# A three-block transformer kernel: the decay matmul's operands padded to 128 rows, and turned 32x32 blocks carried across quadrants by DMA instead of ScalarE

## The reference

```python
def swiglu(h, w_gate, w_up, w_down):
    return (jax.nn.silu(h @ w_gate) * (h @ w_up)) @ w_down
...
        dmat = b[..., :, None] - b[..., None, :] + lii[..., None, :]   # mLSTM, per head
        m_t = jnp.maximum(inter, jnp.max(dmat, axis=-1))
        w_intra = jnp.exp(dmat - m_t[..., None])
        s = jnp.einsum('bhtd,bhsd->bhts', qi, ki) * w_intra
...
    y = jax.nn.sigmoid(o.astype(F32)) * ht * jax.nn.silu(z.astype(F32))
    return y.astype(h.dtype) @ w_out
```

## Time and profile before

| | |
|---|---|
| median of 3 runs (lowest, highest) | 2404.92 us (2404.87, 2405.07) |
| profiled execution, its own time | 2404.78 us |
| its span | 2403.0 us |
| busy: PE, PEld, DVE, ACT, POOL | 99%, 81%, 73%, 55%, 2% |
| granted clock of TensorE | 0.999 of full speed |
| DMA | 578 MB, mean 241 GB/s; 71.5% of the 16 engines on SP's queue |

### The profile page before, as it was taken

How to read it: one execution, slowest core, us unless ns; L and a number is a source line. 1 busy time by engine, 2 the same in 40 slices (tenths; PEclk the granted TensorE clock), 3 DMA queues, 4 the chain that set the end, 5 groups by cost and what they waited for, 6 DMA issues and landing times.

```text
span 2403.0 us, 30577 instructions
## 1 busy us (share of the span) xinstructions
PE 2384.5 (99%) x11017; PEld 1944.2 (81%) x11017; DVE 1747.5 (73%) x2438; ACT 1312.8 (55%) x1913; POOL 44.3 (2%) x67
## 2 busy tenths in 40 slices
PE   9999999999999999999999999999999999999998
PEld 7777888888888888778888888888888778888887
DVE  8885778677787776668778677677776676666665
ACT  6665465545563555545545544555455576655553
POOL 1100000000000000000000000000000000000000
PEclk9999999999999999999999999999999999999999
DMA  8445888788889896567777787777777557776654
GB/s 298 146 132 172 269 294 308 256 305 301 286 313 311 286 316 229 163 222 242 240 238 232 244 273 241 239 239 236 243 245 239 155 186 264 251 240 215 227 194 136
DMA packets 161830, 578.14 MB, mean 241 GB/s; under 512 B 18288, under 2 KB 20592, under 8 KB 161680
## 3 DMA queue, kind: packets, MB, share of 16 engines
q1 hardware_dynamic: 160432, 572.64, 71.5%
q0 software_dynamic: 1104, 3.28, 0.5%
q10 hardware_dynamic: 144, 0.26, 0.0%
HBM read 574.01 MB, written 2.10 MB: 240 GB/s over the span
## 4 chain that ended last, share of the span: by engine, by line
PE 94%; DVE 2%; ACT 2%; issue 1%; DMA 1%; POOL 0%; SPq 0%; DVEq 0%; ACTq 0%
PE PS L1173 30%; PE PS L1175 30%; PE PS L1174 30%; DVE WL L2219 1%; ACT WH L1570 1%; PE PS L916 1%; DMA X<-in_x 0%; PE PS L811 0%; PE PS L884 0%; DVE X L2186 0%; PE PS L1006 0%; PE PS L1074 0%; PE PS L1026 0%; PE PS L1027 0%; PE PS L1023 0%
## 5 line engine op out<-in xcount | busy, mean ns | idle before, releaser
L2219 DVE TENSOR_TENSOR WL<-W,WH 128x1024 fp32r<-128x1024 f32 x814 | 988.9, 1222 | 506.4 <-ACT WH L1570 500.1
L1570 ACT ACTIVATE WH<-W 128x1024 fp32r<-128x1024 f32 x814 | 854.9, 1058 | 720.4 <-PE PS L1175 682.5
L1173 PE MATMUL PS<-WH,XTH 128*128 128x512 f32 x2144 | 853.5, 398 | 3.2 <-DVE XTL L1725 1.2
L1175 PE MATMUL PS<-WH,XTL 128*128 128x512 f32 x2144 | 835.7, 390 | 0.0
L1174 PE MATMUL PS<-WL,XTH 128*128 128x512 f32 x2144 | 835.2, 390 | 0.0
L1173 PEld LDWEIGHTS PS<-WH,XTH 128*128 128x128 f32 x2144 | 402.8, 188 | 93.8 <-issue 10.4
L1175 PEld LDWEIGHTS PS<-WH,XTL 128*128 128x128 f32 x2144 | 402.4, 188 | 85.4
L1174 PEld LDWEIGHTS PS<-WL,XTH 128*128 128x128 f32 x2144 | 402.9, 188 | 83.7 <-issue 3.8
L1173 PE MATMUL PS<-WH,YTH 128*128 128x512 f32 x1120 | 440.2, 393 | 3.5 <-DVE WL L2219 2.4
L1175 PE MATMUL PS<-WH,YTL 128*128 128x512 f32 x1120 | 436.1, 389 | 0.0
L1174 PE MATMUL PS<-WL,YTH 128*128 128x512 f32 x1120 | 436.0, 389 | 0.0
(11 more groups left out here) (287 smaller groups left out, 1182.2 us busy)
## 6 DMA issues: line engine op xcount, KB each, us to landing
W<-in_vec SPq DMA_DIRECT2D x192, 512.0 KB, 4.4
W<-in_avoz SPq DMA_DIRECT2D x192, 512.0 KB, 4.5
W<-in_wg SPq DMA_DIRECT2D x88, 512.0 KB, 5.1
W<-in_wu SPq DMA_DIRECT2D x88, 512.0 KB, 4.8
W<-in_wd SPq DMA_DIRECT2D x88, 512.0 KB, 4.9
W<-in_gate SPq DMA_DIRECT2D x64, 512.0 KB, 4.4
W<-in_aqk SPq DMA_DIRECT2D x64, 512.0 KB, 4.4
W<-in_aout SPq DMA_DIRECT2D x64, 512.0 KB, 4.4
```

The source lines that it names most:

```text
L1173: e.matmul(p, x, WH[:, g % NH, j], start=first, stop=False)
L1175: i = e.matmul(p, y, WH[:, g % NH, j], start=False, stop=last)
L1570: e.activation(WH[:, n % NH], W[:, i % NW], ACT.Copy).then_inc(s_hi, 1)
L2219: e.tensor_tensor(l, src, h.bitcast(F32), ALU.subtract).then_inc(s_lo, 1)
```

## The change

- `M2` and `nsel` have 128 rows instead of 64 (the added rows are zero), and the decay matmul uses them all. DVE instead of ACT writes the high part of M2, straight after the scan that makes MM; the decay matmul of head 0 stands three ticks earlier.
- `TQ` and `MT` get the layouts [p, b, j, t, r] and [p, a, j, t, r]: what goes from quadrant a to b is one run of 1 KB in each partition. The transposes write TQ with strides; the pair copies and low halves read MT and write YTH and YTL with strides (runs of 32 elements). With a scale, the low halves are 8 instructions of 128 elements a partition for 4 of 256.
- The 16 ACT copies of each of the 23 chunks are gone. SP issues 16 transfers, `carry`, each from 32 partitions of TQ to 32 partitions of MT, 1 KB a partition. They come in two parts of 8. `carry_points` places part 0 ahead of stream tile low+7 and part 1 ahead of low+8, where low is the last tile that DVE has lowered when it issues the second transpose. So the wait of part 0 on s_tq stands between two weight issues.
- ACT waits on s_mt >= 256 per chunk before the pair copies: 7 ticks behind the second transpose's tick for ffn (26th tick) and mix, 9 and more for keys, where one copy of 128x1024 then fills KT. DVE's low halves come a tick behind the pairs. DVE waits on s_mt before it writes TQ again; tasks that reuse MID or G1 wait on s_tq instead of s_mt.

```diff
+    for what, *a in score(plan):
+        if what in ("slot", "lower", "fold"):
+            low = max([low] + list(plan.lower[a[0]]))
+        elif what == "start" and a[0] in TURNED:
+            due.append(tick + TURNED[a[0]])
+        elif what == "tick":
+            tick += 1
+            while tick in due:
+                due.remove(tick)
+                number += 1
+                for part in range(2):
+                    points.setdefault(low + NW + 1 + part, []).append((number, part))
...
-        M2 = sb("M2", [64, 384], F32R)
-        nsel = sb("nsel", [64, 8], F32R)
-        MT = sb("MT", [128, 4, 256])
-        TQ = sb("TQ", [128, 2, 512])
+        M2 = sb("M2", [128, 384], F32R)
+        nsel = sb("nsel", [128, 8], F32R)
+        MT = sb("MT", [128, 4, 4, 2, 32])
+        TQ = sb("TQ", [128, 4, 4, 2, 32])
...
-                yield from ticks(0 if h else 3)
                 w.wait_ge(s_mm, 2)
                 w.wait_ge(s_nsel, 4)
-                e.matmul(b[:, 0:384], nsel[:, h:h + 1].to_broadcast([64, 128]), M2[:], start=True, stop=False)
+                e.matmul(b[:, 0:384], nsel[:, h:h + 1].to_broadcast([128, 128]), M2[:], start=True, stop=False)
...
-                yield from ticks(6 if h else 3)
+                yield from ticks(6)
...
             def pairs_T(number, k0, scale):
 
-                w.wait_ge(s_mt, number)
+                w.wait_ge(s_mt, 256 * number)
...
-                yield from ticks(19)
-                yield from quadrants(TQ_FFN + f + 1, MT, 4 if f == 10 else 2, s_mt)
+                yield from ticks(25)
                 w.wait_ge(s_unit, free)
-                yield from pairs_T(MT_FFN + f + 1, 4 * slot, None)
+                yield from pairs_T(TQ_FFN + f + 1, 4 * slot, None)
...
-                yield from blocks_T(MID)
-                yield from ticks(5 if f == 10 else 9)
+                yield from blocks_T(TQ_FFN + f + 1, MID)
+                yield from ticks(7)
                 yield from pair_lows(4 * slot, None)
...
-                yield from ticks(3)
                 w.wait_ge(s_gate, 8)
+                w.wait_ge(s_nsel, 4)
+                e.tensor_copy(M2[0:8, 0:256], MM)
+                e.tensor_copy(M2[0:8, 256:384], MM[:, 128:256]).then_inc(s_mm, 1)
                 w.wait_ge(s_mm, 1)
...
+            def carry(number, part):
+
+                w.wait_ge(s_tq, number)
+                if number > TQ_KEYS + 1:
+                    w.wait_ge(s_kq, number - TQ_KEYS - 1)
+                for a in (2 * part, 2 * part + 1):
+                    for b in range(4):
+                        e.dma_start(MT[32 * b:32 * b + 32, a].rearrange("p j t r -> p (j t r)"),
+                                    TQ[32 * a:32 * a + 32, b].rearrange("p j t r -> p (j t r)")).then_inc(s_mt, 16)
+
             for i, (kind, what, src) in enumerate(stream):
+                for number, part in points.get(i, ()):
+                    carry(number, part)
```

More of the change, by code:

```diff
@@ L487, in score, with carry_points @@
     yield from outproj("Y", fours(YT_BAND), 8, "bout", split=last_rows)
+def carry_points(plan):
+    points, due = {}, []
+    tick = low = number = 0
+    for what, *a in score(plan):
[10 more added lines that the diff above has]
+                    points.setdefault(low + NW + 1 + part, []).append((number, part))
+    return points
 def attention_steps(qready, at, turned):
@@ L1408, in gates @@
                 e.activation(gt, gt2, ACT.Ln, bias=onesf[:, 0:1]).then_inc(s_gact, 1)
[L1409 to L1414, removed]
+                yield from ticks(9)
                 w.wait_ge(s_gate, 9)
@@ L1451, in mix @@
                 if h:
-                    w.wait_ge(s_mt, MT_MIX + h)
+                    w.wait_ge(s_tq, TQ_MIX + h)
                 for t in range(2):
@@ L1458, in mix @@
                 e.activation(SG[:, 512:1024], Gb[ends[3][0]][1][:, :], ACT.Sigmoid).then_inc(s_mixa, 1)
-                yield from ticks(5)
-                yield from quadrants(TQ_MIX + h + 1, MT, 2, s_mt)
+                yield from ticks(10)
                 base = CGH + 4 * h - 4 * (h % 4)
                 w.wait_ge(s_unit, free)
-                yield from pairs_T(MT_MIX + h + 1, 4 * (h % 4), lambda kt: cols[:, base + kt:base + kt + 1])
+                yield from pairs_T(TQ_MIX + h + 1, 4 * (h % 4), lambda kt: cols[:, base + kt:base + kt + 1])
             def qc(n, par, g):
@@ L1475, in keys @@
                 qc(j, par, g)
-                yield from ticks(3 if j else 16)
+                yield from ticks(11 if j else 24)
                 w.wait_ge(s_post, 8)
-                yield from quadrants(TQ_KEYS + j + 1, KT[:, 4 * j:4 * j + 4], 2, s_kq)
+                w.wait_ge(s_mt, 256 * (TQ_KEYS + j + 1))
+                e.activation(by_quadrant(KT, 4 * j, 4), feature_blocks(0, 4), ACT.Copy).then_inc(s_kq, 1)
+                yield
             def values(j, par, g):
@@ L1647, in lows_Y, with blocks_T @@
                 i.then_inc(s_yt, 1)
-            def blocks_T(src):
+            def blocks_T(number, src):
+                if number > 1:
+                    w.wait_ge(s_mt, 256 * (number - 1))
                 for t in range(2):
-                    i = e.transpose(TQ[:, t], src[:, t])
+                    i = e.transpose(TQ[:, :, :, t].rearrange("p b j r -> p j b r"),
+                                    src[:, t].rearrange("p (j b r) -> p j b r", j=4, b=4))
                     if t:
@@ L1973, in gates @@
                                 ALU.subtract).then_inc(s_mm, 1)
-                yield
+                yield from ticks(4)
                 b = full("gate_m")
@@ L2066, in mix @@
                 w.wait_ge(s_mix, at("y1"))
-                w.wait_ge(s_mt, MT_MIX + h)
-                yield from blocks_T(G1)
-                yield from ticks(9)
+                yield from blocks_T(TQ_MIX + h + 1, G1)
+                yield from ticks(7)
                 base = CGH + 4 * h - 4 * (h % 4)
```

38 lines of the change are left out of this document (18 added, 20 removed).

## The result

The changed kernel takes 2452.15 us (median, 2450.84 to 2452.74) beside 2404.89 us before: a ratio of 1.0195, 95% interval 1.0182 to 1.0207, so 47 us slower. The profiled execution has a span of 2450.8 us, 47.8 us more than before.

What follows compares the result with a forecast made beforehand. TensorE was taken as the bound, so time changes only where it idles or a weight comes late. From 2404.8 us, -2.0 -1.3 +0.65 +3.7 = +1.05 gave 2405.8 us; range 2400.5 to 2419.

Steps and rivals of the forecast that it cites:

- What bounds the kernel: Whole kernel: TensorE, busy 99% of the span, is the bound; work taken from ScalarE, busy 55%, isn't.
- The padding: Decay matmul, 8 times: 128 rows instead of 64 save 0.25 us each, -2.0 us in all.
- f=10: Chunk f=10: ScalarE's copies made TensorE idle before two matmuls; removing them gives -1.3 us if the carry comes in time.
- M2: Chain before L1006: two copies move to DVE while TensorE waits for that chain, +0.65 us.
- The landing: Each chunk's 16th carry: there 9.85 us after the transpose, at 0.475 us an issue; bounds 7.9 and 12.
- When it is needed, and what lateness costs: ScalarE's wait for s_mt before the pair copies: late weights in f=4-6 (0.65 us each) and five chunks (0.35 each), +3.7 us.
- the eight chunks that I named: f=4, 5, 6, losing 0.65 us each, and f=0, 1, 2, h=2 and 5, losing 0.35 each; already on the edge.
- other eleven carries, the keys among them: Carries outside the eight chunks on the edge: 1 us or more left before they cost time.
- the carry is late: Rival, wait for s_mt with WH behind it: 16 us lost (2418) landing at 11 us, 2437 at 12; chance 0.29.
- Weights behind the carry cost 0: SP's queue: weights issued behind the carries come late but cost 0, at most 0.5 us for each of the first three chunks.
- Small transfers hold the DMA engines: Rival: each 32 KB transfer occupies the engines 0.8 us, landing at 15, all 19 stall, about 2490; chance 0.03.

Runs made afterwards that it cites:

- the split: The changed kernel with transfers 1 to 8 of each chunk issued by SyncE and 9 to 16 by GpSimd: 2405.86 us, ratio 1.0002.
- the kernel with 128x256 bytes: The changed kernel with 16 transfers per chunk of 128 partitions x 256 bytes, straight across, values wrong: 2453.17 us, ratio 1.0200.
- 12 transfers: The changed kernel with 12 transfers per chunk instead of 16, same 512 KB, part of the crossing left out: 2410.30 us, ratio 1.0025.
- 8 transfers: The changed kernel with 8 transfers per chunk of 64 partitions x 1 KB, same bytes, straight across, values wrong: 2402.42 us, ratio 0.9989.
- the one with copies three ticks early: Against the kernel with eight transfers of 64 partitions per chunk: pair copies and low halves of ffn and mix 3 ticks earlier; 2445.30 us, ratio 1.0175.
- the one with four: Against the kernel with eight transfers of 64 partitions per chunk: pair copies and low halves of ffn and mix 4 ticks earlier; 2490.69 us, ratio 1.0359.
- the old kernel with idle transfers: The kernel before, ScalarE making the quadrants, with SyncE also issuing the 16 transfers per chunk into a tile nobody reads: 2416.58 us, ratio 1.0048.
- GpSimd with late copies: The changed kernel with all 16 transfers issued by GpSimd, pair copies and low halves 4 ticks later (f=10 kept): 2426.45 us, ratio 1.0086.
- 4 transfers: The changed kernel with 4 transfers per chunk of 128 partitions x 1 KB, same bytes, straight across, values wrong: 2401.86 us, ratio 0.9987.
- the mixed split: The changed kernel, M2 by ScalarE; f=3 to 9 carried by SyncE with copies 4 ticks later, other 16 chunks half SyncE, half GpSimd: 2402.92 us, ratio 0.9993.

## Why the prediction was wrong

**What bounds the kernel** held: TensorE stayed at 98%, and 149 us less work on ScalarE bought nothing by itself.

**The padding** held: -2.0 forecast, -1.9 measured. In the changed kernel L1025 (L998 before) starts 0.22 behind its forerunner, and the second weight matmul 0.53 behind L1025 instead of 0.72:

```profile
1813.23 0.39 PE L1202 MATMUL PS<-WH,XTL 128*128 128x512 f32 x1
1813.45 0.33 PE L1025 MATMUL PS<-M,nsel 128*128 128x384 f32 x1
...
1813.98 0.39 PE L1201 MATMUL PS<-WL,XTH 128*128 128x512 f32 x1
```

The weight loads of the two matmuls, in the kernel before and in the changed one, show what the rows change:

```profile
1765.82 0.18 PEld L998 LDWEIGHTS PS<-M,nsel 64*128 64x128 f32 x1 [0.35 <-issue]
```
```profile
1813.23 0.19 PEld L1025 LDWEIGHTS PS<-M,nsel 128*128 128x128 f32 x1
```

The load with 64 rows starts together with its own matmul (1765.82), so nothing of it is hidden; the one with 128 rows starts 0.22 ahead of its matmul (1813.45). The load itself takes 0.182 us with 64 rows and 0.188 with 128. The rule of the Trainium skill that I weighed (TensorE: Matmul & The Clock Gate, "Step-by-step: what each phase is for"), that the row count doesn't matter for a load, agrees with these two lengths. What I drew from it, a gain of 0, does not: the cost lies in the load's start, not in its length.

**f=10** was half right. The first idle time went. In place of the second came a wait of 1.69 us for the low halves, which the late carry held up. With the carry in time both went, as the split shows (1.4 us by its starts against 1.3 forecast). The keys gave 0.7 us more that I had not counted.

**M2** held in the changed kernel: 2.3 instead of 1.6 us before the qk matmul (L1033 now, L1006 in the earlier trace rows). What I left out is the clock, which fell after this wait in the profiled executions of four kernels and not in the changed one.

**The landing is the step that failed**, and in it one term: the issue. I took 0.475 us from five starts in a row at the kernel's start and had 16x0.475+0.05+2.2=9.85. Measured are 0.63 from start to start and 1.9 us to landing, with the weight between the parts 16x0.63+1.9=12.0; single long issues bring it to 13.1 and once 13.4. My upper bound was 12, and my argument for 0.475 was that bytes don't count. For the issue that holds between shapes, as the kernel with 128x256 bytes showed (0.60 against 0.59), but it says nothing of the level. The same queue in the kernel before showed a higher price one line behind those that I used:

```profile
5.09 0.62 SPq L2410 DMA_DIRECT2D W<-in_qkv  x1
5.75 0.54 SPq L2412 DMA_DIRECT2D YA<-in_xt  x1
```

At 0.66, the pitch of the first of these two, the landing comes out at 12.8. The length of the row is not the reason for the higher price: it is there from the second carry on, with two in a row as with eight, while eight issues in a row at the start held 0.42 to 0.49. Nor is the kind of transfer all of it, since the first weight behind eight carries takes 0.58 too and the next two 0.43 (f=5, 633.42 to 634.52). What sets it stays open, and from the kernel before it could only be bounded: between 32 us and its end no two issues stand back to back there.

**When it is needed, and what lateness costs**, held. With each chunk's measured landing the chain gives 24.7 us for the eight chunks that I named and, from 10.85 us on, 17.1 for the other eleven: 41.8 us of stall. By the starts of TensorE's weights the eight lost 26.7; all 19 lost 48.6, and 50.5 without the padding's gain. With 0.7 for M2 and 3.4 for the clock (below) 45.9 are accounted for, and some 5 us stay open, in which late weights may have a part. (The "other eleven carries, the keys among them" are eleven without the keys, fifteen with them; no term hangs on it.) The rival "the carry is late" is what happened, with its place (WH behind the wait for s_mt) and its start: 12 transfers, going on at 9.6 to 11.1 us, lose 8 against 8 transfers. But it had 0.29 of the chance, and its 2437 at 12 us was low by the next two points. Since eight chunks stood at the edge and the slope behind it was 8 to 19 us a microsecond, the range should have followed the bound of the landing (12) and not its favoured value.

**The clock** had no term. The windows of the changed kernel show TensorE's granted clock partly at the lower level twice, where the kernel before has 1.00 from 10 to 2390 us:

```profile
684.00:690.00 6.00, 5.11 (x16) 4.07 (x17) 6.00 (x8) 4.16 (x6) 0.00 (x0) 0.72 0.93 337
1425.00:1431.00 6.00, 6.00 (x21) 4.75 (x20) 6.00 (x9) 2.69 (x3) 0.00 (x0) 0.72 0.94 290
```

At 0.72 over 6 us, 1.7 us of full speed are missing in each, 3.4 in both. The starts say the same. At the lower level a 512-column matmul follows its forerunner by 0.4 to 0.5 us instead of 0.227. There are 60 such distances before (at a clock of 1.00, so for other reasons), 78 in the changed kernel, 88 in the one with copies three ticks early and 170 in the one with four; what they exceed 0.227 by sums to 12.2, 15.8, 17.8 and 34.3 us. So the clock has some 3.5 us of the change's loss, but 17 of the 45 us between the kernels with 7.6 and 9.3 us of stand.

**Weights behind the carry cost 0** was wrong as a sentence of its own: 12 us in the old kernel with idle transfers. f=0 to 2 lose, where SyncE has three weights to issue in the first 6.1 us behind the transpose and not two, and six of the heads, which have three or four; why h=3 and 7, with as many, lose nothing (0.00 and 0.07) stays open. In the changed kernel they are hidden but for the 5 us above at most, and the zero stood by luck. They came out as soon as the stand was removed, which is why moving the copies later gave back 19 us only.

**Small transfers hold the DMA engines** is out: the split loses nothing outside GpSimd's pause, and GpSimd with late copies nothing in f=0 to 7. The rule of the Trainium skill that I named for it (DMA: Bandwidth & Descriptors, "Rules for kernel authors"), to coalesce since a small transfer is mostly overhead, holds here in another place than I had put it: the overhead sat in the issuing queue. 16 transfers of the same 512 KB cost 50 us over 8, through the landing that they delay and not by themselves.

## What to carry to other kernels

When work is moved from an engine to a DMA queue, price the transfers by their number times the pitch of issues in a row, add the landing, and compare the landing with the place in the waiting engine's queue, not with the time at which the data is used: what is queued behind the wait sets the cost. If some ten places stand at the edge of such a wait, the loss grows by tens of microseconds for one, and the range of a forecast must follow the worst price of an issue. If the old kernel has no such row of issues, as here, its price is not known, and one run that adds them idly would have shown it. Moving half of the issues to a second queue was worth more than the later place of the copies, because it mends the landing and the weights behind it at once.

## What the runs showed of the hardware

- A carry's issue from SyncE takes 0.59 to 0.60 us (median) and 0.63 to 0.64 from start to start, for 32x1 KB, 64x1 KB and 128x256 bytes alike; the first of a row takes 0.47 to 0.51, single ones up to 2.08 us. The issue of a 512 KB weight shows 0.33 where nothing is right ahead of it.
- The same transfer from GpSimd is issued in 0.50 us but lands later with 16 a chunk (median 4.8 us against 2.4; with 8 from each queue 3.2 from either), and the queue paused for 5.5 to 7.3 us behind the 133rd, 218th and 303rd of 368 carries (85 apart), and for 3.3 and 6.3 us behind the 109th of 184 and of 128. What it waits for no profile shows.
- The 64-row decay matmul between 128-row ones costs 0.27 to 0.29 us more than one padded with zero rows. Its weight load starts only with the matmul; a 128-row one starts 0.22 us ahead of it.
- TensorE's granted clock fell after one idle time and not after another like it: 0.68 over 3 us after 2.26 us idle with padding and M2, 1.00 after 2.30 in the changed kernel. It also fell after 2.23, 2.28 and 1.83 us in the kernels with 8 transfers, 4 transfers and the mixed split (0.57, 0.57 and 0.59 over 1033 to 1037 us), and not after 2.27 in the even split (1.00 over 1034 to 1037). I found nothing that tells them apart.
